# Encoder layer: loads of the next stage issued in the stage before, waits for last stores moved, sample heads and sample tiles taken first

## The reference, cut to what matters

```python
def encoder_layer(x, ...):                       # x: (1, 1024, 1024) and (1, 512, 1024), float32
    h = rmsnorm(x, norm1_g)
    proj = h @ w_in                              # columns: x1, x2, v (512 each), q, k, v, o, gates
    cp = dwconv3(proj[..., :CONV_CH], conv_w, conv_b)
    kspec = hyena_filter_spectrum(S, ...)        # spectra of two long filters for each channel
    y_hy = hyena_mix(x1, x2, hv, kspec, hy_bias) # twice: gate * (long convolution + bias)
    hm = mlstm_bidir(q, k, v, gates)             # 4 heads x 128, forwards and backwards
    y_ml = sigmoid(o) * norm(hm) * ml_norm_g
    x = x + concat([y_hy, y_ml]) @ w_out
    h = rmsnorm(x, norm2_g)
    u = dwconv3(h @ w_up, ffn_conv_w, ffn_conv_b)
    return x + (silu(gate) * val) @ w_down       # then a final rmsnorm
```

## Time and profile before

| | |
|---|---|
| runs | median 2459.97 us of 3 (2458.02 to 2462.74) |
| the profiled execution | 2459.39 us, its span 2457.4 us |
| PE busy | 2284.2 us (93%) |
| DVE, ACT, POOL busy | 1191.9, 781.2, 148.4 us |
| mean granted TensorE clock | 0.974 |
| DMA | 307.22 MB, mean 125 GB/s |
| stage one | 0 to 767 us |
| stage two | 767 to 1200 us |
| stage three | 1200 us to the end |

### The profile page before, as it was taken

One profiled execution on the slowest core, in us unless ns is written; L12 is line 12 of the kernel. 1 busy time (PEld: TensorE's weight loads), 2 busy tenths in 40 slices (PEclk: granted clock), 3 DMA queues, 4 the chain that ended last, 5 costly groups with the idle time before them and its releaser, 6 DMA issues.

```text
span 2457.4 us, 26109 instructions
## 1 busy us (share of the span) xinstructions
PE 2284.2 (93%) x10340; PEld 1863.8 (76%) x10340; DVE 1191.9 (49%) x1655; ACT 781.2 (32%) x1189; POOL 148.4 (6%) x164
## 2 busy tenths in 40 slices
PE   4999999998995798877599999999999999999998
PEld 3788778887784677766478888888888887888886
DVE  5666676544731667566346433333333333424332
ACT  4422331254432443534225212221222122324221
POOL 0211221100111101010000000000000000000000
PEclk9999999999997999989799999999999999999999
DMA  4344454433444776553645211121111111635442
GB/s 130 99 136 141 133 152 131 131 132 124 122 142 142 271 200 195 176 172 98 222 147 189 91 60 48 60 69 60 60 60 63 57 60 37 210 115 176 152 149 88
DMA packets 212083, 307.22 MB, mean 125 GB/s; under 512 B 15320, under 2 KB 143704, under 8 KB 211706
## 3 DMA queue, kind: packets, MB, share of 16 engines
q1 hardware_dynamic: 199418, 256.00, 34.1%
q0 software_dynamic: 11392, 46.41, 5.1%
q10 hardware_dynamic: 1152, 3.15, 0.3%
HBM read 207.38 MB, written 72.16 MB: 114 GB/s over the span
## 4 chain that ended last, share of the span: by engine, by line
PE 48%; DMA 2%; DVE 1%; ACT 0%; issue 0%; SPq 0%; DVEq 0%; POOL 0%; ACTq 0%
PE mlp_acc L128 10%; PE mlp_acc L129 10%; PE mlp_acc L130 10%; PE mlp_dacc L128 6%; PE mlp_dacc L130 6%; PE mlp_dacc L129 6%; DMA out_s_raw<-y_scratch 1%; PE mlp_acc L2510 0%; DMA mlp_conv_par<-arg_ffn_par 0%; DMA g_scratch<-up_prod 0%; DMA down_d_raw<-arg_w_down_t 0%; DVE out_s_lo L2410 0%; DVE down_d_lo L2450 0%; ACT out_s_hi L2329 0%; DVE up_u L245 0%
## 5 line engine op out<-in xcount | busy, mean ns | idle before, releaser
L128 PE MATMUL mlp_acc<-mlp_h_hi,up_w_hi 128*128 128x512 f32 x1056 | 411.1, 389 | 0.2 <-DVE mlp_h_lo L2430 0.2
L130 PE MATMUL mlp_acc<-mlp_h_hi,up_w_lo 128*128 128x512 f32 x1056 | 410.8, 389 | 0.0
L129 PE MATMUL mlp_acc<-mlp_h_lo,up_w_hi 128*128 128x512 f32 x1056 | 410.8, 389 | 0.0
L2435 DVE TENSOR_TENSOR up_w_lo<-up_w_raw,up_w_hi 128x1024 fp32r<-128x1024 f32 x44 | 53.8, 1226 | 388.3 <-ACT up_w_hi L2346 388.3
L128 PEld LDWEIGHTS mlp_acc<-mlp_h_hi,up_w_hi 128*128 128x128 f32 x1056 | 198.2, 188 | 41.7 <-DVE mlp_h_lo L2430 0.6
L130 PEld LDWEIGHTS mlp_acc<-mlp_h_hi,up_w_lo 128*128 128x128 f32 x1056 | 198.2, 188 | 41.2
L129 PEld LDWEIGHTS mlp_acc<-mlp_h_lo,up_w_hi 128*128 128x128 f32 x1056 | 198.2, 188 | 41.0
L128 PE MATMUL mlp_dacc<-down_d_hi,down_s_hi 128*128 128x512 f32 x528 | 206.4, 391 | 5.4 <-DVE down_d_lo L2450 5.3
L129 PE MATMUL mlp_dacc<-down_d_lo,down_s_hi 128*128 128x512 f32 x528 | 206.1, 390 | 0.0
L130 PE MATMUL mlp_dacc<-down_d_hi,down_s_lo 128*128 128x512 f32 x528 | 206.0, 390 | 0.0
L2346 ACT ACTIVATE up_w_hi<-up_w_raw 128x1024 fp32r<-128x1024 f32 x44 | 46.6, 1059 | 460.1 <-PE mlp_acc L130 460.1
(11 more groups left out here) (240 smaller groups left out, 3908.1 us busy)
## 6 DMA issues: line engine op xcount, KB each, us to landing
in_w_raw<-arg_w_in_t SPq DMA_DIRECT2D x58, 512.0 KB, 3.6
down_s_raw<-g_scratch SPq DMA_DIRECT2D x48, 512.0 KB, 4.3
up_w_raw<-arg_w_up_t SPq DMA_DIRECT2D x44, 512.0 KB, 3.5
g_scratch<-up_prod POOLq DMA_DIRECT2D x22, 768.0 KB, 3.5
filt_tab<-arg_fwd SPq DMA_DIRECT2D x32, 512.0 KB, 4.0
mix_classes<-mix_split SPq DMA_DIRECT2D x48, 256.0 KB, 5.0
mix_kf<-k_scratch SPq DMA_DIRECT2D x48, 256.0 KB, 2.9
mix_split<-mix_classes SPq DMA_DIRECT2D x48, 256.0 KB, 4.8
```

The source lines that it names most:

```text
L128: pe.matmul(out, w_hi, x_hi, start=first, stop=False)
L129: pe.matmul(out, w_hi, x_lo, start=False, stop=False)
L130: return pe.matmul(out, w_lo, x_hi, start=False, stop=last)
L2435: dve.tensor_tensor(w_lo[i % 2][:, :, :], raw[i % 2][:, :, :], w_hi[i % 2][:, :, :].bitcast(F32), ALU.subtract).then_inc(sem["w_low"], 1)
```

## The change

A class `Ahead` allocates, before stage one and for all three, the z buffers, tables, masks, columns and the w_out buffer, and semaphores that are not cleared between stages. In stage one SP runs `load_ahead` behind the load of weight tile n0 + 19. It loads there what stage two loaded first, and both inner tables. POOL's and SP's last waits of stage one go; SP waits for the stores (`all_stored`) at the start of stage two and behind the shuffles of stream 0. The waits for constants move from the start of the engines' lists to the first use. The jobs run sample before prompt (`for s in (1, 0)`). In stage two SP loads all of w_out behind the shuffles back of stream 1, and the first two `so_raw` tiles (of the sample) behind the store of head job 6. The waits for y stores go from the end of stage two to SP in stage three, behind two more operand loads. Stage three takes the token tiles in the order 8 to 11, 0 to 7, and the first product of the up projection its chunks likewise.

```diff
+    def load_ahead():
+        sp.wait_ge(sem["exp_done"], 4)
+        sp.dma_start(fade_d, fade[:, :]).then_inc(sem["g_stored"], 16)
+        sp.wait_ge(sem["multiplied"], n0)
+        for b in range(2):
+            sp.wait_ge(stored[b], 16 * len(range(b, n0 + 1 + N_MIX, 2)))
+        for s in range(len(SEQS)):
+            sp.dma_start(ahead.otab[s][:, :, :], outer_tab[s]).then_inc(ahead.otab_loaded, 16)
+        for st, (s, half, z) in ((0, (0, 0, ahead.z[0])), (2, (1, 0, ahead.z[1][:, 0:nts[1], :])), (3, (1, 1, ahead.z[1][:, nts[1]:, :]))):
+            sp.dma_start(z[:, :, :], token_rows(tok_d, s, 2 * HY + half * HC, HC)).then_inc(ahead.z_loaded[st], 16)
+        sp.dma_start(ahead.mask[:, :, :], masks).then_inc(ahead.const_loaded, 16)
+        sp.dma_start(ahead.gm[:, :], ml_gain).then_inc(ahead.const_loaded, 16)
+        sp.wait_ge(sem["g_stored"], 96)
+        for j in range(4):
+            sp.dma_start(ahead.cols[j][:, :, :, :], cols_d[j]).then_inc(ahead.const_loaded, 16)
+        for d in range(DIRS):
+            sp.dma_start(ahead.fade[:, d, :, :], fade_d[...]...).then_inc(ahead.const_loaded, 16)
+        for s in range(len(SEQS)):
+            sp.dma_start(ahead.tab[s][:, :, :, :, :], inner_tab[s]).then_inc(ahead.tab_loaded[s], 16)
...
     for step in order:
         if step[0] in loads and step not in started:
             loads[step[0]](*step[1:])
-    sp.wait_ge(sem["exp_done"], 4)
-    sp.dma_start(fade_d, fade[:, :]).then_inc(sem["g_stored"], 16)
-    sp.wait_ge(sem["g_stored"], 96)
+        if step == ("load_w", n0 + N_MIX + 7):
+            load_ahead()
...
-    pool.wait_ge(stored[0], 16 * ((n + 1) // 2))
-    pool.wait_ge(stored[1], 16 * (n // 2))
...
-    jobs = [(h, s) for h in range(HEADS) for s in range(len(SEQS))]
+    jobs = [(h, s) for h in range(HEADS) for s in (1, 0)]
...
+    def load_out_weights():
+        for st in (2, 3):
+            sp.wait_ge(y_stored[st], 16 * (HC // P))
+        for n in range(KD):
+            sp.dma_start(ahead.wo_raw[:, n, :, :], w_out[...]).then_inc(ahead.wo_loaded[n], 16)
+
+    def load_first_outputs():
+        sp.wait_ge(head_stored[1], 16 * HEADS)
+        for st in (2, 3):
+            sp.wait_ge(y_stored[st], 16 * (HC // P))
+        for b in range(2):
+            t = SEQS[1][0] // P + b
+            sp.dma_start(ahead.so_raw[b][:, :, :], y_d[...]).then_inc(ahead.so_loaded[b], 16)
...
+    all_stored(first_stored)
     sp.wait_ge(sem["const_set"], 2)
     load_head(0)
-    load_z(2)
-    load_z(3)
     for step in schedule:
         if kind == "split":
             shuffle_classes(*args)
             if args == (0, 0, nts[0] - 1):
-                for s in range(len(SEQS)):
-                    sp.dma_start(tab[s][:, :, :, :, :], inner_tab[s]).then_inc(tab_loaded[s], 16)
-                    if s == 0:
-                        for g in range(ring):
-                            load_k(g)
+                all_stored(total_stored)
+                for g in range(ring):
+                    load_k(g)
                 load_head(1)
...
         elif kind == "back":
             shuffle_split(*args)
+            if args == (0, 1):
+                load_out_weights()
...
             if 0 < args[0] < len(jobs) - 1:
                 load_o(args[0] + 1)
+            if args[0] == len(jobs) - 2:
+                load_first_outputs()
-    for s in range(len(SEQS)):
-        sp.wait_ge(head_stored[s], 16 * HEADS)
...
-    for st in range(len(streams)):
-        act.wait_ge(y_stored[st], 16 * (HC // P))
...
+    first_s = SEQS[1][0] // P
+    tile_at = list(range(first_s, TT)) + list(range(first_s))
+    chunk_at = [tile_at[CH // P * c] * P // CH for c in range(NCH)]
...
-    load_wo(0, 0)
-    load_so(0, 0)
-    load_wo(0, 1)
+    load_so(0, 2)
+    load_so(0, 3)
     sp.dma_start(gain[:, :], g...).then_inc(sem["gain_loaded"], 16)
     sp.dma_start(cp[:, :, :], conv_par).then_inc(sem["par_loaded"], 16)
-    started = [("load_wo", 0, 0), ("load_so", 0, 0), ("load_wo", 0, 1)]
+    sp.wait_ge(ahead.head_stored[0], 16 * HEADS)
+    for st in range(2):
+        sp.wait_ge(ahead.y_stored[st], 16 * (HC // P))
+    started = [("load_so", 0, t) for t in range(4)]
...
     act.wait_ge(sem["eps_set"], 1)
-    act.wait_ge(sem["par_loaded"], 16)
```

182 lines of the change are left out of this document (106 added, 76 removed).

## The result

The changed kernel takes 2446.8 us (median of five runs; 2443.4 to 2449.0), the kernel before 2460.0. The ratio is 0.9945, interval 0.9934 to 0.9956: 13.2 us faster, where 27.4 were forecast. The time lies outside the forecast's own 2426 to 2440 and inside the wide range of 2419 to 2448, near rival B's 2445, but only in part for B's reasons. The profiled execution of after took 2446.0 us with a span of 2444.1. Of all runs in this document only two of e10's six were slow (2640 and 2631 us, mean granted clock 0.84, where its other four took 2416 to 2419), and no median or ratio here rests on them.

What follows compares the result with a forecast made beforehand. TensorE bounds the long product stretches, so gains lie in its waits, longest at the two stage joints. 0 + 14.4 + 7 - 9.5 + 2 - 0.5 + 14.0 = 27.4 us off gives 2432.6 at the median, range 2426 to 2440 (0.55).

Steps and rivals of the forecast that it cites:

- rival B: Stage two: spectrum loads stay late and the new head order gives nothing back; 2445 us, chance 0.22.
- Part 2: First joint: first exponential 9 us from stage start, not 23.4; 14.4 us gained, bounds 8 to 16.
- Part 4: Input stage: moved loads stand in front of weight tile 49, TensorE stops; 9.5 us lost, bounds 13 to 4.
- Part 3: Early stage two: tables and first z leave the crowded queue, spectrum waits shrink; 7 us gained, bounds 0 to 8.2.
- Part 5: Stage two: sample heads first, same work in another order; 2 us gained, bounds -6 and +8.
- Part 6: Stage two: output weights (4.2 MB) loaded there, beside the joins; 0.5 us lost, bounds 3 to 0.
- Part 1: End of stage one: POOL's waits for last stores go, its drain remains; 0 gained, bounds 0 to 1.9 us.
- Part 7: Second joint: earlier stage start 12.0 us, no wait for tile 4 2.0; 14.0 us gained.
- Rival A: Input stage: the stall before weight tile 49 doesn't come; 2423 us, chance 0.14.
- about 6 us: Second joint: expected time between the two stages' matmuls, as a sign that the forecast holds.
- C: First joint: first head still lands 18.7 us after the start; 2459.5 us, chance 0.05.
- D: Input stage: moved loads run at 150 GB/s, TensorE stands 45 us; slower, 2471 us, chance 0.04.

Runs made afterwards that it cites:

- e10: Changed kernel with output weights behind step (1,1)'s class shuffles, inner tables behind the last weight tile, second head's load early, mask waiting for max rows alone: 2416.8 us.
- e2: Changed kernel with all loads for the next stage issued behind the last weight tile instead of behind weight tile 48: 2435.5 us.
- e12: Kernel before with one edit, the heads run sample first in each pair: 2457.3 us.
- e3: Changed kernel with the heads in the old order and the first two output operands loaded behind the last head's store: 2449.1 us.
- e7: Changed kernel with the second head's load, and the wait for input-stage stores, moved up right behind the first head's load: 2442.0 us.
- e9: Changed kernel with output weights later, second head's load early, moved loads behind the last weight tiles, mask waiting for max rows alone, gaps of 14: 2439.1 us.
- e11: Changed kernel with only the two inner tables (4.7 of 7.5 MB) moved behind the last weight tile: 2436.0 us.
- e5: Changed kernel with POOL's waits for its last input-stage stores put back at that stage's end: 2448.3 us.
- e1: Changed kernel with the 4.2 MB of output weights queued behind the last class shuffle of step (1,1), not behind step (0,1)'s split shuffles: 2439.7 us.
- e6: Changed kernel with the planned gaps of head work before the joins of steps (0,1) and (1,1) raised from 9 to 14 units: 2455.9 us.
- e8: Changed kernel with the eight output-weight loads put back at the start of the last stage, in front of its other loads: 2450.4 us.

## Why the prediction was right or wrong

The sum failed in three steps, and parts 2 and 4 were mis-sized (by 4.7 and 3.4 us). Part 3 counted on 7 us from a stop that part 5 removes anyway. Part 5 put the late load of the second head at "some 2 us"; its two stops were 10.5. Part 6 put the output weights at 0.5 and they cost 7.6, since part 5 had taken away the work that would have covered them. The three have one root: the parts were priced one by one against the old trace and then added.

The measured sizes below are by the table above; what is gained is plus. The 2.1 us of drift in front of M belong to no part.

**Part 1**, forecast 0, measured +1.9. The step that failed took two sums that agreed (5.95 and 6.16) for a law. Both kernels' drains stood behind a wait for the store, so the two rows could not tell a fixed end from a fixed length. In the runs the drain lasted 3.65 us from a start behind the landing, 4.23 from the issue, and, when the store landed late (e2), until 1.9 us behind the landing. The upper bound was the value.

**Parts 2 and 3**, forecast 14.4 + 7, measured 7.7 in S-b1: the largest miss, 13.7 us. Here is S-b1 in two parts, before and behind the first spectrum tile x (TensorE's first product into `mix_xacc`), in us:

```
                    S-x   x-b1
before             59.5   37.8
e12_before_order   65.8   39.8
e3_order_back      53.8   33.9
after              49.8   39.9
e7_head1_early     42.3   38.5
e10_four           38.3   39.8
```

The stretches from x to b1 of before, e12 and after (us, TensorE busy, granted clock, DMA share, GB/s):

```profile
827.04:864.86 37.82, 28.42 (x124) 0.91 0.55 190
```

```profile
836.39:876.17 39.78, 36.68 (x190) 0.89 0.24 76
```

```profile
830.38:870.23 39.85, 36.80 (x190) 0.89 0.27 80
```

*Part 2* lies in S-x: 9.7 gained of 14.4. The first exponential came at 13.4, not 9; from 23.4 that is 10.0, inside the bound of 8. The head's v landed 7.3 us behind its own issue (at 9.3 from the start, where I had 6.5 for all). The other 1.28 is ScalarE's table load for the exponential. The kernel before had it too, but there it was done 11.3 us before the mask was ready:

```profile
778.30 1.28 ACT L1857 ACT_TABLE_LOAD   x1
```

In the changed kernel it stands behind the wait for the mask, at 792.66. So it is in after, e3, e7, e9 and e10; in before and e12 it is in the shadow of that wait. Among the changed kernel's edits is the one that put the wait for constants directly in front of this exponential. That this moved the table load is the likely cause; no run tests it alone.

*Part 3* failed. The stop of 5.52 is gone, but x-b1 is 2.0 longer, not 7 shorter. In e12 the tables are still loaded in the crowded stretch and TensorE's longest such wait from x to b1 is 1.3 us as well: with sample heads first more head work stands between the spectrum tiles (190 matmuls for 124). What the moved loads give from x to b1 is 3.9 us in the old order (e3 against before) and nothing in the new one (39.9 for 39.8). In front of x they give 5.7 in the old and 16.0 in the new order.

The second head is the rest. It is now the large one (2.5 MB, a 4.6 us mask), and was still loaded behind the eight class shuffles. The order costs 8.2 of S-b1 with the loads as before (e12) and 1.9 with the loads ahead (after against e3). The two stops in after, 3.9 and 6.6, fall to 3.2 in e7, which gives 8.9 of S-b1 back. e10 gives 11.5, 19.2 of the 21.4 in all, but with a gain that the prediction did not have, a mask that waits for the max rows alone.

**Part 4**, forecast -9.5, measured -12.9 (11.9 to 15.2 by the six executions, so its bound of -13 was about the middle and not the end). Place, cause and rule (bytes in front of the tile at the rate of a full queue) were right, as e11 and e2 show. The term was mis-sized: 10.0 MB moved from 688 to 718 at 334 GB/s, where I had 9.5 MB at 364 and then took less than my own slow end. That the loads began later than 687.8 is mostly the drift of 2.1 us, which moved the tile's own deadline as well. After the stop the clock stood near the level of 1.2 GHz (0.5), as foreseen: six matmuls stand 0.43 us apart, then 0.23. The window behind the stop (us, TensorE busy, granted clock, DMA share, GB/s), where before has 1.00 from 718 to 724:

```profile
718.00:724.00 6.00, 3.65 (x10) 0.57 0.56 152
```

Some 0.9 us more came from matmuls 0.2333 us apart in place of 0.2287 until the stage's end. e5 shows it too; e1, e3, e6, e7 and e8, with the same stop, don't. Its cause stays open.

**Rival A** (no stop) did not come in this kernel. The Trainium skill (DMA: Bandwidth & Descriptors, Rules for kernel authors) says to issue early and wait late; for the moved loads themselves the trace agrees, as TensorE's first matmul starts with the stage. The Trainium skill (DMA: Bandwidth & Descriptors, Queues, rings and completion order) also says that each DMA engine consumes descriptors in ring order. The trace agrees: tile 49, issued right behind the tables, landed 15.5 us later. With the tables behind the last weight tile (e11) the rival's gain was real: 10.3 us.

**Part 5**, forecast +2. Alone it is +7.0 in stage two's trace (e12), in time +2.5 (0.2 to 4.7). In the changed kernel, against e3, stage two is 2.6 longer and the joint 5.6 shorter; in time 2 to 3 us are gained, uncertain by as much. So the forecast of +2 fits, but as a balance of larger things that it did not have: two stops for the second head, 10.5 us, and the order's work on the stops of parts 3 and 6.

**Part 6**, forecast -0.5, measured -7.6 in time (e1), -7.0 in stage two (e8). The step said that the class shuffles behind the weights are wanted only for tiles behind the joins. True, and the old order would have covered it (b3-b4 in e3). I costed parts 5 and 6 one by one, and took the cover of part 6 from a trace that had the old order, while part 5 removed that cover.

**Part 7**, forecast 14.0, measured 11.8 (e-f) + 1.5 (f-end). ScalarE started at 1197.81 (forecast 1197.1), TensorE 4.7 us behind it at 1202.54 (1202.3), and no wait for tile 4. This part went as worked out. (The sign "about 6 us" between the stages' matmuls did not follow from it: 1202.3 less the last matmul's 1194.3 is 8.0, and 8.2 was measured.) Its rows:

```profile
1195.42 1.11 ACTq L1907 DMA_DIRECT2D y_scratch<-mix_classes  x2
1197.81 2.01 ACT L2396 ACTIVATE out_s_hi<-out_first_s_raw 128x1024 fp32r<-128x1024 f32 x2 [2.42 <-DVE mlp_eps L2556]
...
1202.54 0.76 PE L128 MATMUL mlp_dacc<-out_w_hi,out_s_hi 128*128 128x512 f32 x1 [7.81 <-DVE out_w_lo L2473]
```

**The misses**: 13.7 (4.7 of part 2 and 9.0 of part 3), 3.4 (part 4), 0.7 (part 7) and 2.1 of drift are 19.9; the other way 1.9 (part 1), and 3.9, as stage two behind b1 gained 5.4 (3.3 - 3.8 + 5.9) where parts 5 and 6 had 1.5. That leaves 14.1, the 27.4 less the 13.3. **Rival B** had nearly the right time (2445) and half of the road. Part 3 gave nothing from x to b1, as it said. But the spectrum loads did not stay late (the 12 issued from 795 to 870 landed in 2.7 us in the median), part 5 by itself did give something back, and B had no price for part 6. Its closeness is in part luck. C and D did not happen. Of the prediction's two signs of being wrong neither came (a stop of 10.4 us, not over 13; 2.6 to 7.0 us by the order, not over 8): they watched the sizes of single parts, and what failed was how the parts meet. The ends of its wide range do not follow from its bounds either: part 4 at -4 gives 2427, not 2419, and B with part 2 at 8 gives 2451, not 2448.

## What to carry to other kernels

A load that is moved ahead is free only if every load behind it in that queue still lands in time. Count the bytes in front of each later load, not only of the next one: here 2.8 MB in front of tile 49 cost nothing and 7.5 MB cost 13 us. At the end of the queue's work look at the last stores too, which cost 3.8 us in e2. Three moves of issue lines and one semaphore turned 13 us gained into 42. Price edits that touch the same stretch together: one may take away the work that hides the other (parts 5 and 6), or the wait that the other was to remove (parts 5 and 3). When a wait is removed, walk on to the next operand in the queue; the second one is often late for the same reason as the first. And a wait that can be filled with work isn't free time if that work, standing alone, runs at the pace of its own chain.

## What the runs showed of the hardware

- POOL's drain behind a store at the end of stage one: 3.65 us when it started behind the landing (2.82 at the end of the program); started at the issue, 4.23 for a store that lands in 2.3 and 6.76 for one that lands in 4.9, so that both end 1.9 us behind the landing. Taking the wait in front of it away gained 1.97 us.
- A 512 KB weight tile landed 15.5 us behind its issue with 4.7 MB of tables just in front of it, 5 us without them (e11), 3.8 before. SP took 12.6 us from the first moved issue to this tile's with the tables and 12.4 without.
- ScalarE's table load took 1.28 us. It was done before the mask was ready in before and e12 (ScalarE then waited 11.3 and 6.0 us more), and came behind the wait for the mask in after, e3, e7, e9 and e10.
- A 512-token head of five 256 KB loads, with nothing in front, landed 4.1 to 7.3 us behind the issues; from 781 to 786, which is from the first issue on, the queue moved 0.69 MB, 139 GB/s, where I had taken 364.
- From run to run the first 680 us, with the same instructions, differed by up to 3 us (679.1 to 682.2).
